# Even layer of a two-block network: lags through device memory, out-projection of the state space half on high and low parts, and a new order of loads and steps

## The reference

```python
hn = rmsnorm(x, even_norm)
q, k, v, u = split(hn @ even_w_in, [512, 640, 768])      # 512, 128, 128 and 512 columns
o_attn = swa_sink_attention(rmsnorm(q), rmsnorm(k), v, sinks)   # window of 128, 8 heads of 64
y = states of 32 groups of 16 channels, 64 complex states each, driven by u, read out by c
y = gelu(y + d_skip * u)
o_ssm = y * sigmoid(y @ w_glu + b_glu)
x = x + concatenate([o_attn, o_ssm]) @ even_w_out        # 1024 x 1024
```

## Time and profile before

| | us |
|---|---|
| median of 3 runs | 1214.45 |
| lowest, highest | 1213.83, 1216.28 |
| the profiled execution's own time | 1217.08 |
| its span, first to last instruction | 1215.4 |
| PE busy in the span | 1187.6 |
| DVE, ACT, POOL busy | 782.8, 588.9, 64.6 |

### The profile page before, as it was taken

One profiled execution on the slowest core, in us unless ns is written; L12 is line 12 of the kernel. 1 busy time (PEld: TensorE's weight loads), 2 busy tenths in 40 slices (PEclk: granted clock), 3 DMA queues, 4 the chain that ended last, 5 costly groups with the idle time before them and its releaser, 6 DMA issues.

```text
span 1215.4 us, 17637 instructions
## 1 busy us (share of the span) xinstructions
PE 1187.6 (98%) x7043; PEld 1025.4 (84%) x7043; DVE 782.8 (64%) x845; ACT 588.9 (48%) x729; POOL 64.6 (5%) x81
## 2 busy tenths in 40 slices
PE   6989999999999999999999999999999999999997
PEld 5876788888899988888888888888889988888886
DVE  6947666666656457666667666667594646766665
ACT  5437544343566655343435434345574545444443
POOL 2110000000003110000000000000011000000000
PEclk8899999999999999999999999999999999999999
DMA  8243555555554446555555556555533534655551
GB/s 204 91 143 109 187 178 193 187 186 194 173 174 140 139 140 207 176 202 176 199 180 174 190 191 194 186 188 175 191 118 125 177 135 128 202 183 197 180 199 70
DMA packets 158119, 206.05 MB, mean 170 GB/s; under 512 B 9832, under 2 KB 131248, under 8 KB 158064
## 3 DMA queue, kind: packets, MB, share of 16 engines
q1 hardware_dynamic: 157616, 204.51, 51.1%
q10 hardware_dynamic: 448, 0.77, 0.4%
HBM read 203.04 MB, written 1.05 MB: 168 GB/s over the span
## 4 chain that ended last, share of the span: by engine, by line
PE 90%; DVE 5%; ACT 2%; DMA 1%; ACTq 1%; issue 1%; SPq 0%; POOL 0%; POOLq 0%; DVEq 0%
PE outp L754 26%; PE acc L694 20%; PE outp L694 19%; PE outp L757 13%; PE acc L805 3%; PE outp L712 1%; PE outp L724 1%; PE outp L1181 1%; DVE w_lo L2172 1%; DVE h_pair L2217 1%; PE outp L859 1%; DMA raw<-in_even_w_in_dram 1%; ACTq L1847 1%; ACT w_hi L1632 0%; ACT h_pair L1693 0%
## 5 line engine op out<-in xcount | busy, mean ns | idle before, releaser
L1632 ACT ACTIVATE w_hi<-raw 128x2048 fp32r<-128x2048 f32 x177 | 339.5, 1918 | 413.3 <-PE outp L757 285.5
L2172 DVE TENSOR_TENSOR w_lo<-raw,w_hi 128x2048 fp32r<-128x2048 f32 x177 | 405.4, 2290 | 177.5 <-ACT w_hi L1632 177.4
L754 PE MATMUL outp<-h_pair,w_hi 128*128 128x512 f32 x1056 | 266.3, 393 | 0.3
L754 PEld LDWEIGHTS outp<-h_pair,w_hi 128*128 128x128 f32 x1056 | 190.9, 189 | 38.9 <-DVE h_pair L2217 4.2
L757 PEld LDWEIGHTS outp<-h_pair,w_lo 128*128 128x128 f32 x1056 | 144.1, 190 | 10.3
L757 PE MATMUL outp<-h_pair,w_lo 128*128 128x256 f32 x1056 | 147.3, 282 | 0.0
L694 PE MATMUL acc<-w_hi,f_hi 128*128 128x512 f32 x352 | 137.5, 391 | 0.0
L694 PE MATMUL acc<-w_hi,f_lo 128*128 128x512 f32 x352 | 137.3, 390 | 0.0
L694 PE MATMUL acc<-w_lo,f_hi 128*128 128x512 f32 x352 | 137.0, 389 | 0.0
L694 PE MATMUL outp<-w_hi,h_pair 128*128 128x512 f32 (+1 forms) x416 | 114.0, 361 | 0.6 <-DVE w_lo L2172 0.3
L2271 DVE TENSOR_REDUCE arena<-outp 128x256 f32<-128x512 f32 x88 | 56.7, 686 | 59.8 <-PE outp L757 57.5
(11 more groups left out here) (334 smaller groups left out, 1441.2 us busy)
## 6 DMA issues: line engine op xcount, KB each, us to landing
raw<-in_ffn_w_gate_dram SPq DMA_DIRECT2D x44, 1024.0 KB, 5.3
raw<-in_ffn_w_up_dram SPq DMA_DIRECT2D x44, 1024.0 KB, 5.4
raw<-in_ffn_w_down_dram SPq DMA_DIRECT2D x44, 1024.0 KB, 4.8
raw<-in_odd_w_in_dram SPq DMA_DIRECT2D x12, 1024.0 KB, 5.2
raw<-in_w_in_dram SPq DMA_DIRECT2D x10, 1024.0 KB, 5.1
raw<-in_even_w_in_dram SPq DMA_DIRECT2D x5, 1024.0 KB, 9.1
raw<-in_even_w_out_dram SPq DMA_DIRECT2D x4, 1024.0 KB, 5.9
raw<-in_cross_wk_dram SPq DMA_DIRECT2D x4, 1024.0 KB, 5.9
```

What stands on the lines that cost most here:

```text
L754: nc.tensor.matmul(bank.rearrange("p (a l) -> p a l", l=L), wh[:, c, :], x[:, :, c, :], start=c == 0, stop=c == C - 1, skip_group_check=True)
L1632: A(w_hi[:, slot(u), :], raw[:, u % RAW, :], ACT.Copy).then_inc(w_hi_ready, 1)
L2172: tt(w_lo[:, slot(u), :], raw[:, u % RAW, :], w_hi[:, slot(u), :].bitcast(F32), ALU.subtract).then_inc(w_lo_ready, 1)
```

## The change

What it does:

- **Loads at the start.** The small state space inputs, `b` and `c` are issued by ACT ahead of its first work. SP issues x, constants, gain, and then unit 0. `c` comes in two plain loads (no doubled halves), with a semaphore of its own.
- **PE at the start.** Only `b` is transposed ahead of unit 0 (32 instructions). `c` is turned by 64 plain matmuls with the identity, 64 columns wide, between units 0 and 1.
- **Lags.** `lags` is written to a tensor in device memory in 4 moves, and read back into `m_in` in 8, one for each j; both queues wait for all four writes before they read. Half of unit 3 stands ahead of the lag coefficients. The key transposes follow `convolve(1)`, and the transposes of y stand before the first scores.
- **Out-projection.** `WHOLE` is 6: units 6 and 7 are split. `o_ssm` is split by ACT (`gated_hi`, copied into the float32r tile `m_lo`) and DVE (`gated_lo`). `out_glu(1)` is cut into its two row halves around `probs(0)`. `norm(8)` stands before `out_heads(0)`.

Some lines of the diff are left out where they only rename a semaphore or a bank:

```diff
 NB = 4
-WHOLE = 8
...
+    OUT = plan([("even_b", 2), ("even_u0", 1), ("even_c", 2), ("even_u1", 1), ("even", 3), ("even_sc", 4), ("even_out", 4), ("mem_k1", 1), ("ffn0", 44), ("mem_k0", 1), ("odd", len(ODD_BANKS)),
                 ("odd_out", 4), ("mem_k2", 1), ("ffn1", 44), ("mem_k3", 1), ("ffn2", 44), ("mem_v0", 1), ("mix", 10),
                 ("mem_v1", 1), ("mem_v2", 1), ("mix_out", 4), ("mem_v3", 1), ("cross", 4), ("cross_out", 4),
...
     ACC = plan([("prep_a", 1), ("norm0", 4), ("uc", 8), ("u", 2), ("vt0", 4), ("vt1", 4), ("st", 2), ("sf", 4),
-                ("k", 2), ("jg", 2), ("qk", 2), ("y0", 1), ("kt", 1), ("y1", 1), ("yt", 4), ("sc", 2), ("glu", 2),
+                ("k", 2), ("jg", 2), ("qk", 2), ("y0", 1), ("y1", 1), ("kt", 1), ("yt", 4), ("sc", 2), ("glu", 2),
                 ("pt0", 3), ("pt1", 3), ("pv0", 1), ("pv1", 1), ("norm8", 4),
...
         ssm_loads += [(log_dt, row(a["ssm_log_dt"][0]).to_broadcast([P, G]))]
-        bc_loads = [(bc_nat[G * j:G * j + G, :].rearrange("g (h m) -> g h m", h=2),
+        b_loads = [(bc_nat[G * j:G * j + G, :].rearrange("g (h m) -> g h m", h=2),
                      a[n][0].rearrange("g n p -> g (n p)").unsqueeze(1).to_broadcast([G, 2, 1024]))
                     for j, n in enumerate(["ssm_b_re", "ssm_b_im"])]
-        bc_loads += [(bc_nat[G * j + 64:G * j + 64 + G, :].rearrange("g (p h n) -> g p h n", h=2, n=N)[:, :, h, :],
-                      a[n][0]) for j, n in enumerate(["ssm_c_re", "ssm_c_im"]) for h in range(2)]
-        SSM, BC = len(ssm_loads), len(bc_loads)
-        m_moves = [(j, cc) for j in range(S) for cc in range(4)]
-        M_SP, M_ACT = m_moves[:18], m_moves[18:]
+        c_loads = [(bc_nat[G * j + 64:G * j + 64 + G, 0:N * PC], a[n][0].rearrange("g p n -> g (p n)"))
+                   for j, n in enumerate(["ssm_c_re", "ssm_c_im"])]
+        SSM = len(ssm_loads)
+        lag_rows = nc.dram_tensor("lag_rows", (4 * PC, S * 8 * PC), F32, kind="Internal").ap()
+
+        def lags_out(eng, cc):
+
+            eng.dma_start(lag_rows[PC * cc:PC * cc + PC, :],
+                          lags[32 * cc:32 * cc + PC, :, :, :].rearrange("p s i c -> p (s i c)")).then_inc(lag_out, 16)
+
+        def lags_in(eng, j):
+
+            eng.dma_start(m_in[PC * j:PC * j + PC, :, S - 1 - j:, :, :].rearrange("p a s i c -> p a (s i c)"),
+                          lag_rows.rearrange("(a p) m -> p a m", p=PC)[:, :, 0:(j + 1) * 8 * PC]).then_inc(m_in_done, 16)
...
-            if "even" in running:
-                for dst, src in ssm_loads:
-                    sp.dma_start(dst, src).then_inc(ssm_in, 16)
...
-                for dst, src in bc_loads:
-                    sp.dma_start(dst, src).then_inc(bc_in, 16)
...
-                for j, cc in M_SP:
-                    sp.dma_start(m_in[PC * j:PC * j + PC, cc, S - 1 - j:, :, :],
-                                 lags[32 * cc:32 * cc + PC, 0:j + 1, :, :]).then_inc(m_in_done, 16)
-                sp.wait_ge(m_in_done, 16 * 4 * S)
+                for cc in range(2):
+                    lags_out(sp, cc)
+                sp.wait_ge(lag_out, 16 * 4)
+                for j in (7, 5, 3, 1):
+                    lags_in(sp, j)
+                for j in range(2):
+                    load(u0 + 6 + j, quarter(w_out, 1, j), 512)
                 sp.dma_start(mem_sb, a["mem_2"][0].rearrange("(t p) f -> p t f", p=P)).then_inc(mem_in, 16)
-                for kh in (1, 0):
-                    for j in range(2):
-                        load(u0 + 8 - 2 * kh + j, quarter(w_out, kh, j), 512)
+                for j in range(2):
+                    load(u0 + 8 + j, quarter(w_out, 0, j), 512)
...
-                    for j in range(4):
-                        rows = bc_nat[G * j:G * j + G, :]
-                        ins = flip(outp[:, (OUT["even_bc"] + j) % NB, p * G:(p + 1) * G],
-                                   rows[:, p::PC] if j < 2 else rows[:, p * P:(p + 1) * P], G, G * j)
+                    for j in range(2):
+                        ins = flip(outp[:, (OUT["even_b"] + j) % NB, p * G:(p + 1) * G],
+                                   bc_nat[G * j:G * j + G, p::PC], G, G * j)
                 ins.then_inc(bc_flipped, 1)
-                whole_t(u0, k0, fresh=chunks(0))
-                whole_t(u0 + 1, k0 + 1)
+                whole_t(u0, OUT["even_u0"], fresh=chunks(0))
+                pe.wait_ge(c_in, 16 * 2)
+                for j in range(2):
+                    out_taken(pe, OUT["even_c"] + j)
+                for p in range(PC):
+                    for h in range(2):
+                        for j in range(2):
+                            rows = slice(G * (j + 2), G * (j + 3))
+                            ins = nc.tensor.matmul(outp[N * h:N * h + N, (OUT["even_c"] + j) % NB, p * G:(p + 1) * G],
+                                                   bc_nat[rows, p * N:(p + 1) * N], ident[rows, rows],
+                                                   start=True, stop=True)
+                ins.then_inc(bc_flipped, 1)
...
+                whole_n(u0 + 3, k0 + 3, (1,))
...
-                whole_n(u0 + 3, k0 + 3, (1,))
...
-                def out_glu(j):
-
-                    u = u0 + 6 + j
-                    w = raw[:, u % RAW, :].rearrange("p (c n) -> p c n", n=512)
-                    pe.wait_ge(raw_landed[u % RAW], 16 * (u // RAW + 1))
-                    for t in range(T):
+                def out_glu(j, rows=range(T)):
+
+                    w = w_unit(u0 + 6 + j, 512)
+                    for t in rows:
                         out_taken(pe, ko + 2 * j + t)
                     for cc in range(2):
-                        pe.wait_ge(glu_done, cc + 1)
-                        for t in range(T):
-                            for c in (2 * cc, 2 * cc + 1):
-                                ins = nc.tensor.matmul(outp[:, (ko + 2 * j + t) % NB, :], sig[:, c, t * P:(t + 1) * P],
-                                                       w[:, c, :], start=c == 0, stop=False, skip_group_check=True)
-                    ins.then_inc(w_used, 1)
+                        pe.wait_ge(glu_hi, cc + 1)
+                        for lo in range(2):
+                            if lo:
+                                pe.wait_ge(glu_lo, cc + 1)
+                            for t in rows:
+                                bank = outp[:, (ko + 2 * j + t) % NB, :]
+                                for c in (2 * cc, 2 * cc + 1):
+                                    for part in w[0:1] if lo else w:
+                                        ins = nc.tensor.matmul(bank, m_pair[:, 1, 4 * lo + c, t * P:(t + 1) * P],
+                                                               part[:, c, :], start=c == 0 and not lo and part is w[0],
+                                                               stop=False, skip_group_check=True)
+                    if T - 1 in rows:
+                        ins.then_inc(w_used, 1)
 
                 def values_t(b):
...
                 out_glu(0)
+                out_glu(1, (0,))
                 probs(0)
-                out_glu(1)
+                out_glu(1, (1,))
                 probs(1)
                 values_t(0)
...
                     ins.then_inc(w_used, 1)
+                norm(8)
                 out_heads(0, True)
-                norm(8)
                 out_heads(1)
 
...
+                u0, k0 = UNITS["even"], OUT["even"] - 2
+                for dst, src in ssm_loads:
+                    nc.scalar.dma_start(dst, src).then_inc(ssm_in, 16)
+                for dst, src in b_loads:
+                    nc.scalar.dma_start(dst, src).then_inc(b_in, 16)
+                for dst, src in c_loads:
+                    nc.scalar.dma_start(dst, src).then_inc(c_in, 16)
...
                 for j in range(2):
                     k = ACC["k"] + j
                     written(act, k)
                     A(lags.rearrange("p s i c -> p i s c")[:, 4 * j:4 * j + 4],
                       acc[:, k % NB, :].rearrange("p (i s c) -> p i s c", i=4, c=PC),
                       ACT.Copy).then_inc(acc_free[k % NB], 1)
-                qkv_out(1)
                 act.wait_ge(kz_ready, 1)
                 act.wait_ge(k_ready, 1)
-                for j, cc in M_ACT:
-                    nc.scalar.dma_start(m_in[PC * j:PC * j + PC, cc, S - 1 - j:, :, :],
-                                        lags[32 * cc:32 * cc + PC, 0:j + 1, :, :]).then_inc(m_in_done, 16)
+                for cc in (2, 3):
+                    lags_out(nc.scalar, cc)
+                act.wait_ge(lag_out, 16 * 4)
+                for j in (6, 4, 2, 0):
+                    lags_in(nc.scalar, j)
                 qkv_out(2)
...
-                qk_out(ACC["kt"], k_t, L, 1)
                 y_out(1)
                 nc.scalar.preload_act_table_set("gelu_apprx_tanh_and_others")
+                qk_out(ACC["kt"], k_t, L, 1)
...
+                def gated_hi(j):
+                    act.wait_ge(glu_done, j + 1)
```

(19 more changed lines are left out.)

60 lines of the change are left out of this document (31 added, 29 removed).

## The result

| | before | changed |
|---|---|---|
| median of the runs, us | 1214.47 (6 runs) | 1223.65 (6 runs) |
| ratio, 95% interval | | 1.0068 (1.0059 to 1.0078) |
| profiled execution, us | 1217.08 | 1226.29 |
| its span, us | 1215.4 | 1224.6 |
| its mean granted clock | 0.993 | 0.989 |

The change costs 8.3 us by the ratio (9.2 by the medians). The forecast was 1215.9 with a range of 1211.2 to 1219.8: slower, as the result, but the result lies outside the range. Two executions of one kernel further down (the second of experiment 7), at 1309 and 3587 us, were in the slow state and are left out of its numbers. All of the difference arises before 152 us; the first product of the first ffn moves from 142.74 to 152.01, and the spans differ by 9.2.

A forecast was written before the change was run, and what follows sets the result against it. PE was taken to set the time outside the even layer, whose end shifts the program's end. Terms -1.2 - 1.6 + 3.6 + 0 + 0.7 + 0 = +1.5 on 1214.45 gave 1215.9 us, range 1211.2 to 1219.8.

The forecast's parts named there:

- Start, -1.2: PE's first large product: unit 0 would start at 15.8 instead of 17.01 us, -1.2; ends -3.0 and +0.3.
- `c`, +3.6: Between units 0 and 1: 128 records of `c` matmuls at 28 ns each add 3.6 us; ends 1.9 and 7.9.
- Clock at the start, -1.6: Unit 0 starting without two idle gaps may avoid the low clock: -1.6 us, the middle between 0 and -3.1.
- Lags, 0: Lags through device memory: convolution starts between 79.8 and 81.6, taken as 80.7 us as before, so 0; late write +1.9.
- device memory is late: Rival at PE's wait for `m_in`: landing after 80.7 us goes to the end; +1.9, 1217.8 us; chance 0.23.
- The moved half of unit 3: Ahead of the lag coefficients: its 3.6 us make `lags` ready at 71.1 instead of 67.5; counted within the lags' 0.
- if the clock has another low stretch: One of the listed signs that the forecast is wrong, in PE's granted clock; no size was given.
- Keys, y and first scores, +0.7: After the convolution: `w_glu` comes 12.6 us later instead of 11.86, +0.7; ends -0.5 and +1.5.
- Output projection, 0: Out-projection and after: PE saves 2.7 us, DVE pays 6 us of splits and low parts; net 0, ends -2.0 and +1.5.

The follow-up runs named there:

- the second of experiment 7: The kernel before with the changed output projection and order of keys, y and first scores, ACT copying the keys ahead of its table load; ratio 1.0003.
- experiment 5: Three kernels, each the kernel before with one part changed: start (ratio 1.0009), order of keys, y and first scores (1.0025), output projection (0.9990).
- the first run of 6: The changed kernel with 42 transposes of the identity on PE in front of the wait for `m_in`; ratio 1.0053, median span 1220.6 us.
- experiment 4: The changed kernel with SP waiting for `m_in` before loading units 6, 7 and memory rows (ratio 1.0050), then also with strips read in another order (1.0069).
- experiment 2: The changed kernel with only the lag moves as before (direct), half of unit 3 staying ahead of the lag coefficients; ratio 1.0049.
- experiment 7: The kernel before with the new keys order and 12 filler transposes (ratio 1.0016); then that order, the output projection and an earlier ACT key copy (1.0003).
- experiment 1: The changed kernel with direct lag moves as before and half of unit 3 back behind the lag coefficients; ratio 1.0029, median 1218.75 us.
- experiments 1 and 3: The latter is the changed kernel with only half of unit 3 back behind the lag coefficients, lags still through device memory; ratio 1.0033.

## Why the prediction was wrong, step by step

- *Start, -1.2 and `c`, +3.6.* Unit 0 gained 0.79 us (1.8 in experiment 5, 1.4 in the first run of 6); the term is fair. `c` costs 2.07 us for 128 records, 16 ns each and not 28: its lower end (1.9) was right. The 30 ns a transpose had been read at 13.82, where PE was slow; in the same trace 32 of that shape take 0.69 us at 88.52, 22 ns each. The transposes of `b` did not get shorter (1.95 us for 32, as for all 64 before).
- *Clock at the start, -1.6.* The term rested on a misread row. The granted clock of 1.00 ahead of 16.4 us does not mean that PE ran at that pace: its transposes at 9 us took 3.87 / 16 = 242 ns each, those at 79 us 1.07 / 8 = 134. PE is slow from the beginning till some point that differs between executions of one kernel: three profiles of the kernel before give about 21 to 23 us, two of the changed one 20 and 22. In the profiled pair this was worth -1.1 us, near the -1.6, but that is luck and not the mechanism: no profile shows that the change moves this point. The start as a whole: +0.8 forecast, +1.1 measured by the ratio, +2.2 by the medians.
- *Lags, 0.* This is the step that failed. I had the lags ready at 71.1 (the first write is issued at 71.14) and the writes landed at 74.1 (75.0). But I took 291 or 199 GB/s for the reads, and they moved at 141 GB/s, with the DMA share at 1.03. They take 10.5 us and not 5.6 to 7.4 with the start-up, and PE waits 6.41 us. (Two smaller slips did not decide it: no row shows the 1.5 us of start-up, x's own rows leave 1.2, and 8.40 / 13 is 0.65 and not 0.61.) The rival "device memory is late" named the place and the trigger (from 81.6 on) but priced it at +1.9, since it saw a late write and not slow reads. The rule of the Trainium skill (page "SBUF — State Buffer", section "Door 1: The DMA port swizzle") pointed the right way, to the lower rate, but the estimate of 6.0 us from it is too short as well. By the same section of the Trainium skill 16 partitions reach four ports, so two strips reach eight in either order of experiment 4. That experiment does not test the rule.
- *The moved half of unit 3.* I counted its 3.6 us on the lags' path and let a fast landing pay for them. With the direct moves, coefficient to convolution takes 17.2 us in experiment 2 and 17.4 to 17.8 in the other profiles in which PE waits for them; through device memory it takes 17.3 to 18.6. So neither way is clearly quicker, and the slow reads cost no more than the 32 direct moves did. What failed is that they did not gain the 3.6 us that the forecast had them gain. Even in the kernel before the moves were just in time: its third profile has PE waiting 0.77 us for them. So the 3.6 us went through, 2.5 to 4.3 in time. PE work that had covered the latency of the lags was put in front of it.
- *The clock behind the wait.* Nothing of the sort is in the sum; it stands only as a sign of error ("if the clock has another low stretch"). With the waits of 6.41 and 1.49 us came 6.8 us at half clock each, together 5.4 us in the profiled pair and 1.6 to 3.2 in the timed runs. A wait was priced at its length.
- *Keys, y and first scores, +0.7.* 12.55 us from convolution to `w_glu` at full clock, against 11.86 in the profile of before: +0.7, and the chain was as written (the copy behind the table load, 1.49 idle). Alone, however, the order costs 3.0 us in time. The term was mis-sized by 2.3. The profile of that order alone has half clock behind the wait, which can be part of it; what the rest is stays open (experiment 7).
- *Output projection, 0.* Measured -1.2, inside its ends. The wait before the memory product went, as said, and the others were shorter than I had them (1.12 us before the first product, where I had 1.9, and none for the second parts).

Sum as measured: start 1.1, keys 3.0, projection -1.2 (experiment 1 with the three together: 3.5), half and lags 4.8: 8.3.

## What to carry to other kernels

Before work is moved ahead of the start of a long transfer chain, count what PE has left to do until the chain lands; a shorter issue (2.5 us instead of 11.4) does not make a shorter chain. A new wait of PE can cost more than its length, since half clock can come with it: here 6.8 us at half pace came with a wait of 6.4 and again with one of 1.5. It need not: waits of 1.5 and of 3.4 us in experiments 1 and 3 came without it, so one profile does not price it. Where a change has five parts, try each alone: here one paid and the others hid it.

## What was not expected of the hardware

- Reads of 1.18 MB from device memory into strips of 16 partitions ran at 141 to 154 GB/s with the DMA share at 1.03 to 1.05, where x moved at 291 at a share of 0.79. What fills the engines there was not found.
- Stretches of half clock came in lengths of 3.4 or 6.8 us, and their places differ between executions of one kernel.
- 128 records of products with 32 rows by 64 columns, side by side in four places of PE, took 2.07 us, 16 ns each; 32 transposes of 32 rows in two strips took 1.95 to 1.98 us, as 64 in four did, both where PE was slow.
- The row of the granted clock shows 1.00 up to its first fall, or all through the start where it shows no fall, while PE's pace is half: 4 records of unit 0 a us at 17 us and 7 at 22 us, both at 1.00 (experiment 5).
- With 42 transposes more the program's own time exceeded its span by up to 2.3 us instead of 1.7, with 54 by 2.4 to 3.4. No run tells why.
